# Odd scan of a two-layer trunk: rows of m through HBM into five sets, numerators ahead of states

## The reference

```python
def step(carry, xs):
    C, n, m = carry
    ...
    m_t = jnp.maximum(log_inter, jnp.max(log_d, axis=-1))
    w_intra = jnp.exp(log_d - m_t[..., None])
    w_prev = jnp.exp(log_inter - m_t)
    a = w_intra * jnp.einsum('bthd,bshd->bhts', qc, kc)
    num = (jnp.einsum('bhts,bshe->bthe', a, vc)
           + w_prev.transpose(0, 2, 1)[..., None] * jnp.einsum('bhed,bthd->bthe', C, qc))
    den = a.sum(-1) + w_prev * jnp.einsum('bhd,bthd->bht', n, qc)
    denom = jnp.maximum(jnp.abs(den), jnp.exp(-m_t)).transpose(0, 2, 1)[..., None]
    hc = num / denom
    ...
    C_new = w_p[..., None, None] * C + jnp.einsum('bhs,bshe,bshd->bhed', w_s, vc, kc)
```

## Time and profile before

| what | us |
|---|---|
| median of 3 runs (lowest, highest) | 2333.32 (2333.28, 2334.16) |
| span of the profiled execution | 2332.0 |
| PE busy in the span | 2315.6 (99%) |
| DVE busy | 1570.3 (67%) |
| ACT busy | 949.1 (41%) |

### The profile page before, as it was taken

How to read it: one execution, slowest core, us unless ns; L and a number is a source line. 1 busy time by engine, 2 the same in 40 slices (tenths; PEclk the granted TensorE clock), 3 DMA queues, 4 the chain that set the end, 5 groups by cost and what they waited for, 6 DMA issues and landing times.

```text
span 2332.0 us, 39464 instructions
## 1 busy us (share of the span) xinstructions
PE 2315.6 (99%) x16468; PEld 2236.7 (96%) x16468; DVE 1570.3 (67%) x2385; ACT 949.1 (41%) x1491; POOL 30.6 (1%) x44
## 2 busy tenths in 40 slices
PE   8999999999999999999999999999999999999999
PEld 8999999989789999999999999999999999999999
DVE  6886776658867876776587777676245768467473
ACT  5433423444656523414364243245215355234142
POOL 0000000000001000000010000000000010000000
PEclk9999999999999999999999999999999999999999
DMA  9352544422101344334224344225221012322132
GB/s 301 127 163 96 190 148 145 166 70 64 48 19 55 105 149 140 114 109 156 86 91 157 115 156 152 85 78 173 90 73 46 19 55 73 109 73 91 56 99 73
DMA packets 203194, 251.58 MB, mean 108 GB/s; under 512 B 13106, under 2 KB 180874, under 8 KB 203018
## 3 DMA queue, kind: packets, MB, share of 16 engines
q1 hardware_dynamic: 202594, 248.89, 32.5%
q10 hardware_dynamic: 424, 0.18, 0.0%
HBM read 245.76 MB, written 3.28 MB: 107 GB/s over the span
## 4 chain that ended last, share of the span: by engine, by line
PE 91%; DVE 3%; ACT 2%; DMA 2%; issue 1%; SPq 1%; POOL 0%; DVEq 0%; ACTq 0%
PE banks L1111 80%; PE banks L1264 1%; PE banks L1443 1%; PE banks L1442 1%; PE banks L1441 1%; DMA w_raw<-ffn_w_in 1%; PE banks L1588 1%; PE banks L1600 1%; PE banks L1615 1%; DMA mod_first<-w_mod 1%; SPq L1072 0%; SPq L879 0%; PE banks L1809 0%; DVE w_lo L2658 0%; ACT w_hi L2041 0%
## 5 line engine op out<-in xcount | busy, mean ns | idle before, releaser
L1111 PE MATMUL banks<-b_hi,w_hi 128*128 128x320 f32 x2496 | 775.8, 311 | 2.9 <-DVE b_lo L2833 1.2
L1111 PE MATMUL banks<-b_hi,w_lo 128*128 128x320 f32 x2496 | 771.2, 309 | 0.0
L1111 PE MATMUL banks<-b_lo,w_hi 128*128 128x320 f32 x2496 | 771.2, 309 | 0.0
L1111 PEld LDWEIGHTS banks<-b_hi,w_hi 128*128 128x128 f32 x2496 | 468.5, 188 | 15.8 <-issue 9.6
L2041 ACT ACTIVATE w_hi<-w_raw 128x1024 fp32r<-128x1024 f32 x296 | 310.4, 1056 | 403.2 <-PE banks L1111 228.9
L1111 PEld LDWEIGHTS banks<-b_lo,w_hi 128*128 128x128 f32 x2496 | 468.6, 188 | 0.0
L1111 PEld LDWEIGHTS banks<-b_hi,w_lo 128*128 128x128 f32 x2496 | 468.6, 188 | 0.0
L2658 DVE TENSOR_TENSOR w_lo<-w_raw,w_hi 128x1024 fp32r<-128x1024 f32 x296 | 361.4, 1223 | 152.1 <-ACT w_hi L2041 150.6
L1111 PE MATMUL banks<-hid_hi,w_hi 128*128 128x320 f32 x1664 | 400.1, 311 | 0.5 <-DVE hid_lo L2962 0.5
L1111 PE MATMUL banks<-hid_lo,w_hi 128*128 128x320 f32 x1664 | 396.2, 309 | 0.0
L1111 PE MATMUL banks<-hid_hi,w_lo 128*128 128x320 f32 x1664 | 396.2, 309 | 0.0
(11 more groups left out here) (343 smaller groups left out, 2409.6 us busy)
## 6 DMA issues: line engine op xcount, KB each, us to landing
w_raw<-ffn_w_in SPq DMA_DIRECT2D x176, 512.0 KB, 4.8
mod_grain<-w_mod SPq DMA_DIRECT2D x78, 512.0 KB, 6.0
w_raw<-ffn_w_out SPq DMA_DIRECT2D x64, 512.0 KB, 4.4
last_grain<-w_mod SPq DMA_DIRECT2D x40, 512.0 KB, 5.2
w_raw<-ffn_w_out SPq DMA_DIRECT2D x32, 384.0 KB, 3.6
w_raw<-w_in_odd SPq DMA_DIRECT2D x20, 512.0 KB, 4.7
mod_first<-w_mod SPq DMA_DIRECT2D x6, 1024.0 KB, 11.8
w_raw<-w_in_even SPq DMA_DIRECT2D x12, 512.0 KB, 5.8
```

The lines of the kernel that those rows point to most:

```text
L1111: ins = pe.matmul(o, w3[w], v3[v][cols], start=first and i == 0, stop=last and i == 2, skip_group_check=onto_read)
```

## The change

The rows of m no longer go through PE (`bcast` is gone). Once DVE has made `m_rows`, SP stores them to HBM (`m_all`), waits for that, and fetches for each group the 4 rows of 128 values spread over all partitions, straight into the place of `w_prev`, of which there are now five sets where there were three. Exponents and `w_prev` are made from there. A fetch for group n+5 waits until a_t of group n is made and its state taken. The weight loads of units 12 and 13 go between these fetches, and the stores of the end states behind them.

PE's loop is now `keys_queries(n+2)`, `numerators(n+1)`, `states(n)`, after `keys_queries(0)`, `keys_queries(1)` and `numerators(0)`. Numerators of even groups go to banks 4 and 5, those of odd ones to 0 and 1, group 9 to 2 and 3. The denominators have two sets. The first product of a tile moves from DVE (`finish`) to ACT (`finish_first`, four instructions, groups 0, 2, 3, 4, 5). In groups 4 and 9 (`WHOLE_EXPONENTS`) DVE adds the mask in one instruction and ACT takes the scalar in as a bias, head by head. DVE makes the exponents of groups 0 to 2 ahead of the low parts of the Fourier blocks. The split of unit 11 moves behind the third Fourier block. Some semaphores are shared to make room for the new ones.

```diff
-        w_prev = place("w_prev", [P, SETS, CH, P], at=a0 + 6144)
+        PREV_SETS = SETS + 2
+        w_prev_most = place("w_prev_most", [P, SETS, CH, P], at=a0 + 6144)
+        w_prev_last = place("w_prev_last", [P, CH, P], at=hl + 2048)
+        w_prev_over = place("w_prev_over", [P, CH, P], at=place.at["a_rows"])
+        w_prev = [w_prev_most[:, c] for c in range(SETS)] + [w_prev_last[:, :, :], w_prev_over[:, :, :]]
+        m_all = nc.dram_tensor("m_all", (GR, P), F32, kind="Internal").ap()
...
+        WHOLE_EXPONENTS = [n >= SETS and SEEN[n - SETS] for n in range(NG)]
+
+        def wait_for_m(eng, n):
+
+            c = n % PREV_SETS
+            eng.wait_ge(block_in[c], BLOCK_LOADS[c] + 16 * (n // PREV_SETS + 1))
...
-                for i in range(4):
+                def load_m(n):
+
+                    t, d = GROUPS[n]
+                    if n >= PREV_SETS:
+                        sp.wait_ge(a_ready, n - PREV_SETS + 1)
+                        sp.wait_ge(st_taken, n - PREV_SETS + 1)
+                    r = row_of(t, d)
+                    sp.dma_start(w_prev[n % PREV_SETS].rearrange("p h t -> p (h t)"),
+                                 m_all[r:r + CH, :].rearrange("h t -> (h t)").partition_broadcast(P))\
+                        .then_inc(block_in[n % PREV_SETS], 16)
+
+                for i in range(2):
                     load_mix(OU + 10 + i, wo, KT, slice(256 * i, 256 * (i + 1)))
+                sp.wait_ge(gate_dve, 6)
+                sp.dma_start(m_all[:, :], m_rows[:, 0, :]).then_inc(rows_out, 16)
+                sp.wait_ge(rows_out, 16)
+                sp.wait_ge(w_used, OU + 9 + 1)
+                for n in range(PREV_SETS - 1):
+                    load_m(n)
+                sp.wait_ge(m_turned, 1)
+                load_m(PREV_SETS - 1)
+                load_mix(OU + 12, wo, KT, slice(512, 768))
+                load_m(PREV_SETS)
+                load_mix(OU + 13, wo, KT, slice(768, 1024))
+                for n in range(PREV_SETS + 1, NG):
+                    load_m(n)
 
...
+                    elif n == 1:
+                        pe.wait_ge(k_kept_act, 4)
+                        pe.wait_ge(k_kept_dve, 3)
                     elif n < NG - 1:
-                        pe.wait_ge(h_done, n)
+                        pe.wait_ge(h_done, n - 1)
...
+                pe.wait_ge(k_kept_act, 3)
+                pe.transpose(bank[2][:, GR:2 * GR], m_rows[:, 1, :], ident[0:GR, 0:GR]).then_inc(m_turned, 1)
                 token_transform(0)
                 context_transform()
-                pe.wait_ge(k_kept_act, 3)
-                pe.transpose(bank[2][:, GR:2 * GR], m_rows[:, 1, :], ident[0:GR, 0:GR]).then_inc(m_turned, 1)
-                bcast(0)
-                bcast(1)
                 token_transform(1)
-                bcast(2)
+                keys_queries(0)
                 token_transform(2)
-                keys_queries(0)
                 token_transform(3)
+                keys_queries(1)
+                numerators(0)
                 for n in range(NG):
+                    if n + 2 < NG:
+                        keys_queries(n + 2)
                     if n + 1 < NG:
-                        keys_queries(n + 1)
-                    numerators(n)
-                    if n + SETS < NG:
-                        bcast(n + SETS)
+                        numerators(n + 1)
                     states(n)
...
+                def finish_first(n):
+
+                    t, _ = GROUPS[n]
+                    act.wait_ge(den_ready, n + 1)
+                    if n > 0:
+                        act.wait_ge(h_done, n)
...
+                act.wait_ge(m_turned, 1)
+                act.activation(e_m[:, :], bank[2][:, GR:2 * GR], ACT.Exp, scale=-1.0).then_inc(e_m_ready, 1)
                 token_high(0)
+                weights(0)
                 act.wait_ge(four_ready, 2)
                 act.activation(hid_hi[:, 4:8, 0:T_CTX], bank[3][:, :].rearrange("p (g t) -> p g t", g=D_GROUPS), ACT.Copy,
                                scale=(T_CTX * D_DIM) ** -0.5).then_inc(four_hi, 1)
-                act.wait_ge(m_turned, 1)
-                act.activation(e_m[:, :], bank[2][:, GR:2 * GR], ACT.Exp, scale=-1.0).then_inc(e_m_ready, 1)
-                weights(0)
+                weights(1)
                 token_high(1)
-                weights(1)
+                weights(2)
                 token_high(2)
-                weights(2)
+                split(11)
                 token_high(3)
                 for n in range(SETS):
                     values(n)
-                for n in range(SETS, NG):
-                    weights(n)
-                    values(n)
-                act.wait_ge(state_stored, 16 * 4)
+                for n in range(NG):
+                    if not SEEN[n]:
+                        finish_first(n)
+                    if n + SETS < NG:
+                        weights(n + SETS)
+                        values(n + SETS)
...
-                    dve.wait_ge(bcast_ready, n + 1)
+                    wait_for_m(dve, n)
                     if n >= SETS:
                         dve.wait_ge(a_ready, n - SETS + 1)
                         if n - SETS in STATE_GROUPS:
                             dve.wait_ge(v_ready, n - SETS + 1)
-                    for h in range(CH):
-                        r = row_of(t, d, h)
-                        ins = dve.scalar_tensor_tensor(out=w_intra[:, n % SETS, h, :],
-                                                       in0=bank[BCAST_BANK[n % SETS]][:, h * P:(h + 1) * P],
-                                                       scalar=ab[:, 0, r:r + 1], in1=masks[:, d, :],
-                                                       op0=ALU.subtract, op1=ALU.add)
+                    tile, m_rows_of = w_intra[:, n % SETS, :, :], w_prev[n % PREV_SETS]
+                    if WHOLE_EXPONENTS[n]:
+                        ins = dve.tensor_tensor(tile, m_rows_of, masks[:, d, :].unsqueeze(1).to_broadcast([P, CH, P]), ALU.add)
+                    else:
+                        for h in range(CH):
+                            r = row_of(t, d, h)
+                            ins = dve.scalar_tensor_tensor(out=tile[:, h, :], in0=m_rows_of[:, h, :], scalar=ab[:, 0, r:r + 1],
+                                                           in1=masks[:, d, :], op0=ALU.subtract, op1=ALU.add)
                     ins.then_inc(x_ready, 1)
...
+                for n in range(SETS):
+                    exponents(n)
                 token_low(0)
                 dve.wait_ge(four_hi, 2)
                 dve.scalar_tensor_tensor(out=hid_lo[:, 4:8, 0:T_CTX], in0=bank[3][:, :].rearrange("p (g t) -> p g t", g=D_GROUPS),
                                          scalar=(T_CTX * D_DIM) ** -0.5, in1=hid_hi[:, 4:8, 0:T_CTX].bitcast(F32),
                                          op0=ALU.mult, op1=ALU.subtract).then_inc(four_lo, 1)
-                exponents(0)
-                exponents(1)
                 token_low(1)
-                split(11)
-                exponents(2)
                 weigh(0)
                 token_low(2)
+                split(11)
                 token_low(3)
                 for n in range(NG):
                     if n + 1 < NG:
                         weigh(n + 1)
                     invert_den(n)
-                    finish(n)
+                    if SEEN[n]:
+                        finish_second(n)
                     if n + SETS < NG:
                         exponents(n + SETS)
```

123 lines of the change are left out of this document (59 added, 64 removed).

## The result

| | before | after |
|---|---|---|
| time, median (us) | 2333.74 (2333.28 to 2335.47, 4 runs) | 2356.82 (2355.91 to 2359.78, 4 runs) |
| span of the profiled execution (us) | 2332.0 | 2358.0 |
| mean granted clock of the span | | 0.994 |
| q_w of group 1, start (us) | 1792.73 | 1791.59 |
| q_w of group 9, start (us) | 1828.82 | 1853.15 |

The ratio is 1.010, 95% interval [1.0088, 1.0112]. The forecast was 2347.3 us with 2341 to 2353 as its range, so direction and place were right and the size was not. The profiled execution of after is its slowest one, 2359.78 us, 3.0 above the median.

A forecast was written before the change was run, and what follows sets the result against it. PE was taken to bound the kernel, with DVE nearly full beside it in the scan. Loop +15.4 us and head -1.4 gave +14.0: span 2346.0, time 2347.3 us, range 2341 to 2353.

The forecast's parts named there:

- direction and place: Slower, in the scan's loop over groups: PE and DVE wait for each other in every turn, +15.4 us.

## What to carry to other kernels

When two engines hand work to each other in a loop, write the order of both as a ring and add up what lies between one engine's result and the wait that needs it in the same turn. Blocks that wait for nothing new belong ahead of the block that waits; a result used one turn later costs nothing, and the same result used at once cost up to 2.5 us a turn here. When the sum says that TensorE will now rest, don't carry over the durations from a schedule in which it never did: price the blocks at both clock levels, give the lower one a real chance, and read the level from the spacing of the matmuls, not from the clock column alone. And before a wait is moved on a queue, list all that is queued behind it: one load ahead of four stores held PE up for 10 us.
